# Rebuilding the first stage of a two-layer diffusion backbone: when its inputs are loaded, how the adaLN weights are shared out, and where the activations are normalised

## The reference, cut to what matters

```python
def ada_mod(cond, w, b):
    m = (jax.nn.silu(cond) @ w + b)[..., None, :]
    return jnp.split(m, 3, axis=-1)          # shift, scale, gate
...
for i in range(DEPTH):
    shift, scale, gate = ada_mod(c, ada_w[i], ada_b[i])
    h = rmsnorm(x, norm_w[i]) * (1 + scale) + shift
...
# attention of the latent tokens, one head
bias = rpb[:, dr_idx[None, :, None], dc_idx[:, None, :]]
s_loc = jnp.where(col_in[:, None, :], s_loc + bias[None], -jnp.inf)
```

## Time and profile before

| | us |
|---|---|
| three runs | 3042.96, 3038.2, 3044.3 |
| span of the profiled execution | 3035.0 |
| PE busy | 2776.8 (91%) |
| DVE busy | 1887.6 (62%) |
| ACT busy | 1375.1 (45%) |
| POOL busy | 577.0 (19%) |

### The profile page before, as it was taken

The page is one execution under the profiler, slowest core; times in us unless marked ns, Lnnn a source line. Parts: engine busy times, 40 slices in busy tenths (PEclk is TensorE's granted clock), DMA queues, the critical chain, the costliest instruction groups (busy, mean ns, idle before and its releaser), DMA issues. The chain is left out here.

```text
span 3035.0 us, 51975 instructions
## 1 busy us (share of the span) xinstructions
PE 2776.8 (91%) x17133; PEld 2680.1 (88%) x17133; DVE 1887.6 (62%) x3054; ACT 1375.1 (45%) x2263; POOL 577.0 (19%) x716
## 2 busy tenths in 40 slices
PE   2459999999998799999999999898999999998797
PEld 2458999999998789999999999898999999997797
DVE  3888888888843555666566656435556655665333
ACT  1033344334333545565556555324555655555422
POOL 3312222222111121122112211102211221122011
PEclk9999999999999799999999999999999999999799
DMA  8556666666643222112112222333211221121042
GB/s 239 189 198 223 232 229 229 227 233 231 220 146 117 104 81 70 65 66 69 63 65 68 69 67 66 132 124 111 74 58 66 69 69 62 62 73 45 4 165 91
DMA packets 115499, 362.09 MB, mean 119 GB/s; under 512 B 29056, under 2 KB 31232, under 8 KB 114560
## 3 DMA queue, kind: packets, MB, share of 16 engines
q1 hardware_dynamic: 69408, 252.74, 24.4%
q0 software_dynamic: 21200, 87.04, 8.6%
q10 hardware_dynamic: 24848, 21.76, 2.6%
HBM read 345.76 MB, written 15.73 MB: 119 GB/s over the span
## 5 line engine op out<-in xcount | busy, mean ns | idle before, releaser
L445 PE MATMUL bank<-h_hi,w_hi 128*128 128x384 f32 x2576 | 964.4, 374 | 49.0 <-DVE h_lo L1106 34.3
L447 PE MATMUL bank<-h_hi,w_lo 128*128 128x384 f32 x2576 | 872.8, 339 | 0.0
L446 PE MATMUL bank<-h_lo,w_hi 128*128 128x384 f32 x2576 | 870.1, 338 | 0.0
L413 DVE TENSOR_TENSOR w_lo<-raw,w_hi 128x1024 fp32r<-128x1024 f32 x418 | 542.3, 1299 | 436.1 <-ACT w_hi L405 399.6
L405 ACT ACTIVATE w_hi<-raw 128x1024 fp32r<-128x1024 f32 x418 | 442.1, 1060 | 457.2 <-PE bank L447 428.9
L445 PEld LDWEIGHTS bank<-h_hi,w_hi 128*128 128x128 f32 x2576 | 491.6, 191 | 72.2 <-issue 45.4
L446 PEld LDWEIGHTS bank<-h_lo,w_hi 128*128 128x128 f32 x2576 | 492.5, 191 | 13.5 <-issue 7.2
L447 PEld LDWEIGHTS bank<-h_hi,w_lo 128*128 128x128 f32 x2576 | 488.3, 190 | 0.0
L1071 DVE SCALAR_TENSOR_TENSOR ada_terms<-raw_ada,cond_rows 128x1024 f32<-128x1024 f32 x256 | 312.7, 1221 | 11.2 <-DMA raw_ada<-in_late 6.7
L445 PE MATMUL bank<-y_hi,w_hi 128*128 128x384 f32 x768 | 262.8, 342 | 29.2 <-DVE y_lo L1176 22.0
L446 PE MATMUL bank<-y_lo,w_hi 128*128 128x384 f32 x768 | 261.8, 341 | 0.0
(11 more groups left out here) (216 smaller groups left out, 4410.7 us busy)
## 6 DMA issues: line engine op xcount, KB each, us to landing
raw<-in_stream SPq DMA_DIRECT2D x482, 512.0 KB, 3.3
raw_ada<-in_late POOLq DMA_DIRECT2D x128, 512.0 KB, 3.7
x_kept<-y POOLq DMA_DIRECT2D x2, 3072.0 KB, 9.8
y<-x_kept POOLq DMA_DIRECT2D x2, 3072.0 KB, 10.2
bias<-in_rpb ACTq DMA_DIRECT2D x16, 256.0 KB, 6.2
S<-in_state ACTq DMA_DIRECT2D x16, 256.0 KB, 2.6
out_state_out<-s_out ACTq DMA_DIRECT2D x16, 256.0 KB, 2.1
y<-in_x ACTq DMA_DIRECT2D x1, 3072.0 KB, 21.0
```

What stands on the lines that cost most here:

```text
L413: nc.vector.tensor_tensor(w_lo[:, mk % SPLIT_SLOTS, :], raw[:, raw_n % RAW_SLOTS, :], w_hi[:, mk % SPLIT_SLOTS, :].bitcast(F32), ALU.subtr ...
L445: nc.tensor.matmul(bank[:, 0:T], w_hi[:, slot, w], hi[:, kt, :], start=kt == 0, stop=False)
L446: nc.tensor.matmul(bank[:, 0:T], w_hi[:, slot, w], lo[:, kt, :], start=False, stop=False)
L447: last = nc.tensor.matmul(bank[:, 0:T], w_lo[:, slot, w], hi[:, kt, :], start=False, stop=kt == KT - 1)
```

## The change

- `start`: ACT issues three DMAs only, `cond_rows`, `cond` and x, with a semaphore of their own for the conditioning, and then applies SiLU. POOL issues the six small inputs.
- The attention bias comes ready from the host as one array of 16 heads. In each turn of `na` POOL loads the bias of one head (256 KB) first, waits for it and adds the mask (one instruction on 128 x 512) before its third `raw_ada` load. DVE waits for the mask ahead of its addition.
- `ADA_HALVES` alternates DVE and PE throughout, in 4 groups of 16: 32 halves each. DVE takes the shift tiles, PE the scale tiles, so each group ends with what four tiles k need. At a group's end DVE waits for PE's last half and makes the group's `gain`.
- `squares0`, `norm0` and `mod0` are gone as phases. PE sums the squares in group 1, after its fourth half. DVE, ACT and POOL normalise and split k = 0 to 7 between the halves of group 2, and 8 to 11 in group 3; 12 to 15 follow after group 3. The three weight halves of `na` are no longer split ahead: half 0 is split before k = 12, halves 1 and 2 after k = 15.
- `ada` is written out instead of a loop of two turns.

```diff
-ADA_GROUPS = 2
-ADA_HALVES = ([(e, t, half) for pair in range(3) for half in range(2) for e, t in (("dve", pair), ("pe", pair))]
-              + [("dve", t, half) for t in (3, 4) for half in range(2)])
-ADA_TILES = {"dve": 5, "pe": 3}
+ADA_GROUPS = 4
+ADA_TILES = KT // ADA_GROUPS
+MODULATE_AT = {(2, 2 * k + 1): k for k in range(8)} | {(3, 4 * k + 2): 8 + k for k in range(4)}
+ADA_HALVES = [(e, t, half) for t in range(ADA_TILES) for half in range(2) for e in ("dve", "pe")]
+TOTAL_AT = (1, 7)
...
             def ada(pe, phase, turn):
                 for g in range(ADA_GROUPS):
-                    wait_steps(pe, turn, ("dve", f"mods{g}", True))
+                    if g >= 2:
+                        wait_steps(pe, turn, ("dve", f"mods{g - 2}"))
                     for k, (engine, tile, half) in enumerate(ADA_HALVES):
                         if engine == "pe":
                             slot = raw_wait(pe, phase, turn, 16 * g + k)
-                            ada_half(banks[4 + g], raw[:, slot, :], tile, half).then_inc(consumed[slot], 1)
+                            ada_half(banks[4 + g % 2], raw[:, slot, :], tile, half).then_inc(consumed[slot], 1)
+                        if (g, k) == TOTAL_AT:
+                            wait_steps(pe, turn, ("pool", f"added{KT - 1}"))
+                            sum_squares(pe, phase, turn)
...
+            def ada(act, phase, turn):
+                squares_of_x(act, turn)
+                norm(act, phase, turn)
+                for k in range(KT):
+                    if k % ADA_TILES == 0:
+                        wait_steps(act, turn, ("dve", f"gain{k // ADA_TILES}"))
+                    if k == KT - ADA_TILES:
+                        split_hi(act, "na", 0, 0)
+                    wait_steps(act, turn, (("dve", "pool")[k % 2], f"scaled{k}"))
+                    if k >= 2:
+                        wait_steps(act, turn, ("dve", f"lo{k - 2}"))
+                    shift(act, turn, 0, k)
+                for k in range(1, LOOKAHEAD):
+                    split_hi(act, "na", 0, k)
...
             def ada(dve, phase, turn):
+                before = None
                 for g in range(ADA_GROUPS):
...
+                        if (g, k) in MODULATE_AT:
+                            scale_and_split(turn, MODULATE_AT[g, k])
                     half_used(dve, phase, turn, before)
+                    before = None
+                    ada_group(phase, turn, g)
+                    if g == ADA_GROUPS - 1:
+                        split_lo(dve, "na", 0, 0)
+                for k in range(KT - ADA_TILES, KT):
+                    scale_and_split(turn, k)
+                low(turn, KT - 1)
+                for k in range(1, LOOKAHEAD):
+                    split_lo(dve, "na", 0, k)
+
+            def ada_group(phase, turn, g):
+                at = ADA_TILES * g
+                add_bias(turn, at, ADA_TILES, ada_sums[:, g % 2, :, 0, :], ada_sums[:, g % 2, :, 1, :], f"halves{g}")
+                half_used(nc.vector, phase, turn, 16 * g + 15)
...
+            def scale_and_split(turn, k):
+                if k == 0:
+                    wait_steps(dve, turn, ("act", "rstd"))
+                if k % 2 == 0:
+                    if k >= 2:
+                        wait_steps(dve, turn, ("act", f"shifted{k - 2}"))
+                    done("dve", f"scaled{k}", nc.vector.tensor_tensor(scaled[:, 0, :], x[:, k, :], rstd[:], ALU.mult))
+                if k >= 1:
+                    low(turn, k - 1)
...
             def na(dve, phase, turn):
...
-                            wait_steps(dve, turn, ("pe", f"scores{r}"))
+                            wait_steps(dve, turn, ("pe", f"scores{r}"), *([("pool", "masked")] if r else []))
...
             def na(pool, phase, turn):
...
+                wait_steps(pool, turn, ("dve", "biased2", True))
+                lone()
+                pool.dma_start(bias[:], dram["bias"][bass.ds(turn, 1)].rearrange("a p r k -> p (a r) k")).then_inc(s["bias_in"], 16)
                 load_ada(0)
                 load_ada(1)
...
+                pool.wait_ge(s["bias_in"], 16 * (turn + 1))
+                lone()
+                masks = K["grid"][:, 0:GRID_W].unsqueeze(1).broadcast_to([P, 2 * ROWS, GRID_W])
+                b = bias[:].rearrange("p r (i k) -> p (r i) k", i=ROWS)
+                done("pool", "masked", nc.gpsimd.tensor_tensor(b, b, masks, ALU.add))
```

131 lines of the change are left out of this document (59 added, 72 removed).

## The result

| | before | after |
|---|---|---|
| median of the runs, us | 3042.24 (4 runs) | 2971.86 (4 runs, 2970.79 to 2978.18) |
| ratio | | 0.9776, 95% interval 0.9762 to 0.9789 |
| span of the profiled execution | 3035.0 | 2976.6 |
| first adaLN operation of DVE | 50.47 | 20.46 |
| end of the adaLN stage | 199.65 | 155.5 |

70 us less, 2.24%; 2973 was forecast. The profiled execution after is itself the slowest of the four (2978.18, 1.6 above its span).

The account below looks back on a forecast made before the run. PE was taken to bound the steady turns, so only the program's head could shrink: 30.8 + 22.9 + 17.8 - 1.2 = 70.3 us off the 3035.0 span gives 2964.7, plus 8.0 for the median, 2973; range 2960 to 2996.

Parts of the forecast that it names:

- Start: Program head: conditioning loaded first on ACT's queue, so DVE's adaLN work begins at 19.7 instead of 50.5; 30.8 us less.
- Stage: adaLN weight halves, from DVE's first operation to the last half: 126.3 us instead of 149.2, 22.9 less.
- I take 3.7: adaLN, after POOL's adds: a pair of one DVE and one PE half takes 3.7 us, for 15 pairs.
- stage paced by landings: Rival, adaLN: weight-half landings set the pace at 4.43 us a pair, 14 us more, 2987; chance 0.17.
- the prediction's own signs: Profile checks: DVE starting near 20 us, groups 1 and 3 at 3.6 to 3.8 a pair, first `raw_ada` landed near 164.5.
- wrong if the pair is 4.4: Failure sign, adaLN: the forecast is wrong if one DVE half and one PE half take 4.4 us together.
- Overlap and tail: Twelve tiles k made beside halves in groups 2 and 3; tail to the first `raw_ada` landing 18.5 us, not 36.3.
- overlap doesn't work: Rival, groups 2 and 3: engines stall on each other, tiles cost 1.45 each as before, 17 us return, 2990; chance 0.05.
- Heads: Turns of `na`: per-head bias load and mask cost 0 a turn, and 1.2 us once in the first head.
- heads slower: Rival, turns of `na`: mask and issue not absorbed by DVE's free 4.8 us, 19 to 30 more, 2992 to 3003; chance 0.10.
- The rule weighed: DVE and POOL's shared-port lock: by the rule alone eight POOL multiplications cost DVE 1.2 each, some 5 us over the sum.
- Slower than before: Rival, turns of `na`: bias load delays the third `raw_ada` half; slower if bias lands after 16.2 us; chance 0.03.

Follow-up runs that it names:

- the second profile: The changed kernel run again with nothing changed, profiled a second time: 2972.2 us median, ratio 0.9775 to the kernel before, adaLN stage 131.8 us.

## Why the prediction was right, point by point

The time was right (2973 forecast, 2971.86 measured), and so were direction, range and each mechanism in outline. The sum was less exact than the total: that it hit within 2 us is luck, as the last paragraph of this section shows.

**Start: 19.7 forecast, 20.46 measured, by other means.** The conditioning alone would have let the stage begin at 17.1 (the kernel without the wait for small inputs), 2.6 us earlier than forecast; the small loads, which were to hide behind `cond_rows`, came 3.4 us later than that. Undoing this gained nothing, since the next weight halves weren't there either. The bound behind both is one that the working didn't look at: the third and fourth half, asked for at 2.5 and 3.0 us, landed only at 22.6 and 23.7, as x did (22.5).

**Stage: 126.3 forecast, 135.1 and 131.8 measured.** This is the term that was mis-sized, by 5.5 to 8.8 us. The step that failed is "I take 3.7": it rested on landings of 3.2 to 3.3, read where halves had been asked for at regular distances, and the other stretch, with a median of 4.2, was put down to DVE's runs of four. With strict alternation the landings were 4.4. The rival "stage paced by landings" had the right mechanism; its price of 14 us, 4.43 for each pair, was too high, the slot cycle gives 4.1. The experiments with eight slots show it: the waits go, and the stage takes 111 to 114.

The row that the choice of 3.7 leaned on was also the best of its stretch. PE's idle time of 0.16 stands before the half at 70.03; before the three ahead of it there were 0.74, 0.21 and 0.60. From 58.34 to 70.03 a pair took 3.90, so not even this stretch showed 3.7 (DVE's half took 3.85 in it).

```profile
58.34 3.58 PE L571 MATMUL bank<-cond,raw 128*128 128x2 f32 x16 [0.74 <-DMA raw<-in_stream]
62.13 3.58 PE L571 MATMUL bank<-cond,raw 128*128 128x2 f32 x16 [0.21 <-DMA raw<-in_stream]
66.30 3.58 PE L571 MATMUL bank<-cond,raw 128*128 128x2 f32 x16 [0.60 <-DMA raw<-in_stream]
```

By the prediction's own signs this part came out wrong. Groups 1 and 3 were to take 3.6 to 3.8 a pair with idle times below 0.3, and "wrong if the pair is 4.4". Counted from PE's last half of one group to that of the next, they took 4.36 and 4.58 in the first profile and 4.27 and 4.01 in the second, with idle times up to 3.3. Group 2, put at 4.0, took 3.98 and 4.02.

The Trainium skill (DMA: Bandwidth & Descriptors, "Anatomy of one DMA — SWDGE (gpsimd) path") fits a transfer as about 2.0 us plus its bytes at 436 GB/s. That section is about loads that GpSimd issues, and these are SP's; as an estimate for 512 KB the fit gives 3.2 us. That is the smallest landing here, and not the 4.4 at the median, so as a price for a slot's cycle it is too low by a quarter.

What of the stage was right: without the mask on POOL 15.5 us go (about 17 forecast), and no operation of 9.7 is left.

**Overlap and tail: 17.8 forecast for the tail, 16.9 measured** (36.3 less 19.4). The 17 us at which the rival "overlap doesn't work" was priced are 14 to 16: the tail is 15.6 longer without it. Its tiles were free in the stage, as assumed, though for a reason that makes the stage longer: DVE was waiting anyway (a pair of group 2 took 4.0 with tiles and 4.02 in the kernel without overlap).

**Heads: 0.** A steady turn took 37.50 us before and takes 37.50 after, from POOL's load of `cache_k` to the next one's. The 1.2 us that were put down once, for the first head, aren't there either: from the first `raw_ada` operation to POOL's loads of the next turn it was 33.8 before and is 33.7. The mask on 8 columns confirms the 0; the reserve is smaller than the 4.8 us of DVE's idle time suggested. Two masks more, 2.6 us of POOL's own time, were not absorbed. The idle time counts only where it lies between the mask and `probsT`, which is what the rival "heads slower" said in its condition.

**The rule weighed.** The prediction took DVE's 1.90 under POOL's adds, 0.68 more than its own 1.22, for less than the lock that the Trainium skill states, and set the rule's price aside. That reading was wrong. The turns taken in the kernel with three masks show the same pattern: some 1.1 of DVE and 0.8 of POOL make both DVE's 1.90 and the 1.92 of an add (an add of this size that meets no DVE operation is shown as 0.99 in the changed kernel), and DVE's 9.71 under the long mask is the remainder of that mask from 82.69 on and its own 1.1. The lock holds; an instruction of DVE loses what is left of POOL's when it arrives. It changed the time little here, because DVE was waiting for halves in the stage and had its reserve in the heads.

**Slower than before.** The bias load landed in a median of 2.9 us, where that rival would have needed 16.2.

**From the sum to the median: two errors of the same size cancelled.** Up to the first `raw_ada` operation the sum forecast 71.5 us less; it was 61.1 in the first profile and 64.7 in the second. Behind it nothing of note was changed, yet the rest takes 2799.0 us in the profile of before and 2800.0 to 2802.9 in those changed ones whose heads do the usual work: the profiled execution of before lies low in the scatter. The spans therefore differ by 58.4 only (63.2 against the second profile), the medians by 70.4. The forecast added the 8 us by which the median of before stood over its profiled span. In every execution after for which both are known the time is 1.6 us above the span, so some 6 of the 8 were only the scatter of that one execution; the median after stands 4.7 below its first profile's span and 0.4 above the second's. Taken with the measured 61.1 or 64.7 the same working would have given 2982 or 2978, 6 to 10 us too high.

## What to carry to other kernels

A prefetch ring is sized by its cycle, not by its bandwidth: hold time plus release to issue plus the median landing, divided by the slots that the slowest consumer has, must be under its time for one item (here 8.2 / 2 = 4.1 against 3.4 to 3.6, which is too long, and 8.2 / 4 = 2.05, which is short enough). Use the median landing of a busy stretch, never the smallest. In the head of a program look at what comes second behind each wait before paying to remove the first. And free time of an engine in a turn is worth only what lies before the point at which another engine needs it; add the work once, twice and three times to find the edge.

## What the runs showed of the hardware that was not expected

- The landing of a 512 KB half stayed at a median of 4.4 to 4.5 us whether four or eight slots were in use and the core moved 253 or 314 GB/s. Why it is above the 3.3 of the stretch from 53.5 to 70 before was not settled.
- A load of 16 KB issued 0.4 us behind one of 2 MB on the same queue took 12.4 us; issued ahead of it, 3.4. In the changed kernel, on POOL's queue and as the last of six, 0.5 KB took 15.4 us.
- Holding back x (3 MB) did not bring the conditioning a tenth of a microsecond earlier (it landed at 14.0), but it brought PE's second weight half, asked for at 2.5 us on SP's queue, from 24.5 to 16.1.
- In the stretches read, POOL's additions and DVE's operations with two inputs in SBUF go one after the other, an instruction at a time, and the time of standing is shown as busy time: 1.30 us becomes 2.06 for POOL, 1.22 becomes 2.0 to 2.3 for DVE.
